# Expert order from four tiles, place rules per expert, and a new order of the last stores and of the first expert products in a hybrid step kernel

## What is computed

```
x = x + gate1 * (mixed @ w_o)
h2 = rms_norm(x, norm2_g) * (1 + scale2) + shift2
x = x + gate2 * hier_moe(h2, ...)

def hier_moe(h, ...):                      # 16 experts in 4 groups, d_expert 512
    g_idx = top-1 group of softmax(t @ w_grp + b_grp)
    top_v, top_i = top-2 experts within that group of t @ w_exp + b_exp
    w_top = softmax(top_v) * g_p
    for e in range(16):
        he = silu(t @ w1[e]) * (t @ w3[e])
        y = y + combine[:, e:e+1] * (he @ w2[e])
```

## Time and profile before

| what | us |
|---|---|
| median of 3 runs | 1240.91 |
| lowest and highest | 1238.01, 1241.13 |
| the profiled execution | 1242.69 |
| its span, first to last instruction | 1240.9 |
| TensorE busy | 1166.9 (94%) |
| VectorE busy | 535.8 (43%) |
| ACT busy | 226.4 (18%) |
| POOL busy | 324.3 (26%) |

### The profile page before, as it was taken

How to read it: one execution, slowest core, us unless ns; L and a number is a source line. 1 busy time by engine, 2 the same in 40 slices (tenths; PEclk the granted TensorE clock), 3 DMA queues, 4 the chain that set the end, 5 groups by cost and what they waited for, 6 DMA issues and landing times.

```text
span 1240.9 us, 14438 instructions
## 1 busy us (share of the span) xinstructions
PE 1166.9 (94%) x5748; PEld 713.9 (58%) x5749; DVE 535.8 (43%) x1037; ACT 226.4 (18%) x478; POOL 324.3 (26%) x269
## 2 busy tenths in 40 slices
PE   4899999999999999999999999999957899999795
PEld 1567677777777777777777777645442233333332
DVE  2553378354786682474244426435650211111111
ACT  3221257222570002001100010021201010101000
POOL 0465600378003333333333333000101111121101
PEclk9999999999999999999999999999868899999998
DMA  9844220022200222222222225441299699999964
GB/s 353 309 159 170 88 77 1 18 68 77 78 1 1 68 68 69 68 68 68 68 68 68 68 70 225 176 170 54 85 382 426 267 352 397 409 405 410 402 210 133
DMA packets 52611, 206.52 MB, mean 166 GB/s; under 512 B 3424, under 2 KB 4000, under 8 KB 46352
## 3 DMA queue, kind: packets, MB, share of 16 engines
q1 hardware_dynamic: 47552, 189.39, 39.8%
q0 software_dynamic: 4672, 15.67, 4.5%
q10 hardware_dynamic: 320, 0.53, 0.1%
HBM read 192.51 MB, written 16.29 MB: 168 GB/s over the span
## 4 chain that ended last, share of the span: by engine, by line
PE 84%; DMA 9%; DVE 2%; issue 1%; POOL 0%; ACT 0%; POOLq 0%; DVEq 0%
PE psum L2222 34%; PE psum L2028 12%; PE psum L2392 6%; PE psum L2286 6%; PE psum L2130 4%; PE psum L2456 3%; PE psum L2418 3%; PE psum L2190 3%; PE psum L2006 3%; PE psum L1948 2%; DMA weight_ring<-in_w 2%; PE psum L2470 2%; DMA arena<-in_w 1%; DMA arena<-rows_scratch 1%; DMA arena<-h_scratch,slot_tokens 1%; PE psum L2164 1%
## 5 line engine op out<-in xcount | busy, mean ns | idle before, releaser
L2222 PE MATMUL psum<-arena,weight_ring 128*128 128x320 f32 x928 | 256.9, 432 | 0.0
L2222 PEld LDWEIGHTS psum<-arena,weight_ring 128*128 128x128 f32 x928 | 175.9, 190 | 72.7
L762 POOL TENSOR_TENSOR weight_ring<-weight_ring 128x512 f32<-128x512 f32 x80 | 105.8, 1323 | 353.6 <-DMA weight_ring<-in_w_in 163.7
L2222 PE MATMUL psum<-x,weight_ring 128*128 128x320 f32 x640 | 179.5, 432 | 0.0
L2222 PEld LDWEIGHTS psum<-x,weight_ring 128*128 128x128 f32 x640 | 121.1, 190 | 49.6
L763 POOL TENSOR_TENSOR weight_ring<-weight_ring 128x512 f32<-128x512 f32 x80 | 110.8, 1386 | 0.0
L1533 DVE TENSOR_TENSOR arena<-psum,arena 128x320 f32<-128x320 f32 x124 | 59.4, 488 | 92.4 <-PE psum L2222 91.6
L2028 PE MATMUL psum<-weight_ring,x 128*128 128x256 f32 x384 | 88.0, 380 | 0.4 <-DVE x L1290 0.4
L2028 PEld LDWEIGHTS psum<-weight_ring,x 128*128 128x128 f32 x384 | 71.7, 190 | 11.2 <-issue 1.1
L2392 PE MATMUL psum<-weight_ring,arena 128*32 128x512 f32 x512 | 78.2, 604 | 0.0
L2286 PE MATMUL psum<-weight_ring,arena 128*128 128x512 f32 x160 | 71.5, 596 | 0.0
(11 more groups left out here) (340 smaller groups left out, 1481.6 us busy)
## 6 DMA issues: line engine op xcount, KB each, us to landing
arena<-in_w SPq DMA_DIRECT2D x22, 2048.0 KB, 17.5
weight_ring<-in_w SPq DMA_DIRECT2D x21, 2048.0 KB, 22.6
weight_ring<-in_w_in SPq DMA_DIRECT2D x16, 2048.0 KB, 8.5
arena<-in_w_ada SPq DMA_DIRECT2D x6, 2048.0 KB, 11.6
x<-in_w SPq DMA_DIRECT2D x5, 2048.0 KB
weight_ring<-in_w_ada SPq DMA_DIRECT2D x8, 1024.0 KB, 14.3
x<-in_x_sample SPq DMA_DIRECT2D x2, 2048.0 KB, 12.1
weight_ring<-in_w_conv_out SPq DMA_DIRECT2D x2, 2048.0 KB, 7.9
```

The costliest lines, as they stand in the source:

```text
L762: nc.gpsimd.tensor_tensor(out[:, 0:2], a_[:, 0:2], b_[:, 0:2], op)
L2222: last = mm(product_psum(q, name), w[:, k, :], src[:, k, :], start=(k == 0), stop=(k == 3))
```

## The change

- The counts matmul no longer is a job of its own. `count(4)` stands inside the last `wo` job, after `rank(3)`, and counts four tiles; `expert_order` uses it and runs before the last `residual`. A second `count(5)` gives the full counts for the overflow chunks only.
- The slot of a token is worked out from five numbers per expert (`rank_distance`, `place_rules`: 16 columns each), which are looked up through the masks of all tokens in one product and one sum of `[128, 800]` (`rules_found`); `places` is left with few steps.
- The first table has 12 columns instead of 92, with one-hots of its own for each tile; the 80 overflow columns move to the weight table, which becomes 184 columns wide (`wide_hots`).
- The last tile's `h2` is shifted by VectorE instead of POOL, POOL's product of it is cut into two halves, and its three stores are issued by ACT instead of SP.
- SP starts with the first weight block right after the order and waits for the last `wo` job only after it. Down blocks of couple 0 wait for `s_last_scaled` and `s_h2out`.
- On TensorE the first gate product comes after the first gathered tile; the weight table and the second tile's transposes follow it. The late modulation part is read by VectorE before the weight table.
- `hidden_half(0)` comes before `gate_difference`.

```diff
@@ psum_jobs
+        if j == 2 * NT - 1:
+            jobs.append(("rank", NT - 2, "dve"))
         jobs.append(("wo", j, "dve"))
...
-    jobs += [("rank", last - 1, "dve"), ("x2T", 2 * last + 1, "act"), ("route", last, "dve"), ("rank", last, "dve")]
-    return jobs + [("count", 0, "dve")]
+    return jobs + [("x2T", 2 * last + 1, "act"), ("route", last, "dve"), ("rank", last, "dve")]
@@ sync
-            job_done(sp, "wo", 2 * NT - 1)
-            sp.wait_ge(s_h2, NT)
-            sp.dma_start(h2_dram[P * CTX:P * NT, :], h2[:, CTX, :]).then_inc(s_h2out, 16)
-            sp.dma_start(y_dram[P * CTX:P * NT, :], x_sb[:, D * CTX:D * NT]).then_inc(s_outx, 16)
-            sp.dma_start(y_dram[T:T + P, :], x_sb[:, D * CTX:D * NT]).then_inc(s_outx, 16)
...
                 load_gate_up("gate", "a", t, a)
+                if t == 0:
+                    job_done(sp, "wo", 2 * NT - 1)
                 load_gate_up("gate", "b", t, b)
...
-                if t == 1:
+                if t == 0:
+                    sp.wait_ge(s_x2, 2 * NT)
+                    sp.wait_ge(s_last_scaled, 1)
+                elif t == 1:
                     sp.wait_ge(s_wtable, NT)
@@ gpsimd
-            pool.wait_ge(s_x2, 2 * NT)
-            nc.gpsimd.tensor_tensor(gate1[:, 0, :], x_sb[:, D * CTX:D * NT], mod2[:, 0, 1, :], mult).then_inc(s_last_wide, 1)
-            pool.wait_ge(s_last_scaled, 1)
-            nc.gpsimd.tensor_tensor(h2[:, CTX, :], h2[:, CTX, :], mod2[:, 1, 1, :], add).then_inc(s_h2, 1)
+            for half in range(2):
+                pool.wait_ge(s_x2, 2 * CTX + half + 1)
+                part = slice(512 * half, 512 * (half + 1))
+                nc.gpsimd.tensor_tensor(gate1[:, 0, part], x_sb[:, D * CTX:D * NT][:, part], mod2[:, 0, 1, part], mult).then_inc(s_last_wide, 1)
@@ scalar
             A(h2[:, CTX, :], gate1[:, 0, :], ACT.Copy, scale=stat[:, 5 * NT - 1:5 * NT]).then_inc(s_last_scaled, 1)
+            act.wait_ge(s_x2, 2 * NT)
+            act.dma_start(y_dram[P * CTX:P * NT, :], x_sb[:, D * CTX:D * NT]).then_inc(s_outx, 16)
+            act.dma_start(y_dram[T:T + P, :], x_sb[:, D * CTX:D * NT]).then_inc(s_outx, 16)
+            act.wait_ge(s_h2, NT)
+            act.dma_start(h2_dram[P * CTX:P * NT, :], h2[:, CTX, :]).then_inc(s_h2out, 16)
@@ vector
+            def place_rules():
+                second, near, far, big, start, cap, step, whole_, past, twice = part16
+                V.tensor_scalar(start, far, 128.0, -64.0, mult, add)
...
+            def rules_found():
+                flat = masks.rearrange("p i j e -> p (i j) e")
+                shape = [P, RULES, 2 * NT, EXPERTS]
+                link(V.tensor_tensor(looked, flat.unsqueeze(1).to_broadcast(shape), rules.unsqueeze(2).to_broadcast(shape), mult))
+                link(V.reduce_sum(found.rearrange("p v n -> p (v n)"), looked.rearrange("p v n e -> p (v n) e"), axis=AX))
 
             def places():
...
+                V.tensor_tensor(passed, rank, found[:, 1], ALU.is_ge)
+                V.tensor_tensor(full, rank, found[:, 3], ALU.is_ge)
+                link(V.tensor_tensor(at_, rank, found[:, 0], add))
...
+            def wide_hots(i):
+                if i >= 2:
+                    dve.wait_ge(s_wtable, i - 1)
+                for j in range(2):
...
+            ranks(NT - 2)
+            expert_order()
             residual(2 * NT - 1)
-            ranks(NT - 2)
+            rank_distance()
+            x2_sum(NT - 1)
+            place_rules()
             x2_rstd(NT - 1)
             dve.sem_inc(s_last_rstd, 1)
             choose(NT - 1)
+            dve.wait_ge(s_last_scaled, 1)
+            h2_shifted(NT - 1)
+            rules_found()
             ranks(NT - 1)
-            expert_order()
             places()
...
             hidden(0)
+            hidden_half(0)
             gate_difference()
             slot_gates(0, 0)
-            hidden_half(0)
             rows_made(0)
@@ tensor
+            def count(tiles):
+                pe.wait_ge(s_upto, tiles)
+                mm(count_psum[tiles - NT + 1], ones[:, :], rt[tiles - 1][:, 48:64], start=True, stop=True).then_inc(s_count, 1)
...
+                if j == 2 * NT - 1:
+                    wo_part(j, ps, 1, range(1))
+                    rank(NT - 2)
+                    count(NT - 1)
+                    wo_part(j, ps, 1, range(1, 4)).then_inc(s_job, 1)
...
-            ada_part(LAST_PAIR, late_psum, range(0, 4), late_slot)
+            ada_part(LAST_PAIR, late_psum, range(0, 2), late_slot)
             rank(NT - 1)
...
-            ada_part(LAST_PAIR, late_psum, range(4, 8), late_slot).then_inc(s_late, 1)
+            count(NT)
+            ada_part(LAST_PAIR, late_psum, range(2, 8), late_slot).then_inc(s_late, 1)
...
-            weight_table()
-            next_tokens(0)
             pe.wait_ge(s_late_rows, 1)
...
-            next_tokens(1)
+            next_tokens(0)
             main_gate(0)
+            pe.wait_ge(s_order, 1)
+            weight_table()
...
+            next_tokens(1)
             main_up(0)
```

More of the change, by code:

```diff
@@ L213 @@
             for j in range(len(JOBS))]
+RULES = 5
 PAIRS = 4
@@ L396, in build @@
         square = at(Z + 16816, 256).rearrange("p (a b) -> p a b", a=16)
-        looked = at(Z + 17072, 2 * NT * EXPERTS).rearrange("p (i e) -> p i e", i=2 * NT)
-        ten = [at(Z + 17232 + 10 * n, 2 * NT) for n in range(17)]
+        rules = at(Z + 17072, RULES * EXPERTS).rearrange("p (v e) -> p v e", v=RULES)
+        found = at(Z + 17152, RULES * 2 * NT).rearrange("p (v n) -> p v n", v=RULES)
+        part16 = [at(Z + 17232 + 16 * n, EXPERTS) for n in range(10)]
+        looked = at(Z, RULES * 2 * NT * EXPERTS).rearrange("p (v n e) -> p v n e", v=RULES, n=2 * NT)
+        ten = [at(Z + 1024 + 10 * n, 2 * NT) for n in range(5)]
         hots = sb("slot_one_hots", (NT - 2) * 2 * SLOTS)
@@ L425, in build @@
         pair = [psum[:, 1024 * j:1024 * (j + 1)] for j in range(PAIRS)]
-        table_psum = pair[PAIRS - 1][:, 512:512 + TABLE]
-        weight_psum = pair[PAIRS - 2][:, 512:512 + TABLE]
+        table_psum = psum[:, 3584:3584 + TILES]
+        wide_psum = psum[:, 2560:2560 + 2 * TABLE]
+        count_psum = [psum[:, 2816 + 16 * n:2832 + 16 * n] for n in range(2)]
         shifted_psum = psum[:, 3840:3904]
@@ L1757, in _ @@
                 if j % 2 == 0:
+                    x2_sum(j // 2 - 1)
                     x2_rstd(j // 2 - 1)
@@ L1783, in _ @@
             V.tensor_copy(idx_out[:, :], rows_out[:, :]).then_inc(s_rows_f, 1)
+            dve.wait_ge(s_lateT, 1)
+            late = late_T_psum.rearrange("p (t l v) -> p l t v", t=4, v=2)
+            for lane, n in enumerate(ADA_PAIRS[LAST_PAIR]):
+                last = V.tensor_tensor(mod[:, 8 * n:8 * n + 8].rearrange("p (n v) -> p n v", v=2), late[:, LANE // 2 * lane],
+                                       col("b_ada")[:, 4 * n:4 * n + 4].unsqueeze(2).to_broadcast([P, 4, 2]), add)
+            last.then_inc(s_late_read, 1)
+            dve.wait_ge(s_late_read, 1)
+            V.tensor_copy(rp[:, 3], m6[:, 5]).then_inc(s_late_mod, 1)
+            dve.wait_ge(s_count, 2)
+            V.tensor_copy(counts, count_psum[1])
             dve.wait_ge(s_rexp, 1)
@@ L2278, in _, with wo_part @@
             pe.wait_ge(s_fev, 6 * last_job + 4)
-            def wo_part(j, ps, part):
+            def wo_part(j, ps, part, steps=range(4)):
                 i, n = divmod(j, 2)
@@ L2284, in wo_part @@
                 pe.wait_ge(s_mixT, 2 + 2 * part)
-                for k in range(4 * part, 4 * part + 4):
+                for k in (4 * part + step for step in steps):
                     last = mm(ps[:, 0:512], mixT[:, k, P * i:P * (i + 1)], w[:, k, :], start=(k == 0), stop=(k == KT - 1))
@@ L2319, in table @@
                 for j in range(2):
-                    last = mm(table_psum, slot_hot[i][:, j, :], pair_hot[i % 2][:, j, :], start=(i == 0 and j == 0),
+                    last = mm(table_psum, slot_hot[i][:, j, :], pair_hot[i][:, j, :], start=(i == 0 and j == 0),
                               stop=(i == NT - 1 and j == 1))
@@ L2369, in weight_table @@
                     for j in range(2):
-                        last = mm(weight_psum, slot_hot[i][:, j, :], pair_hot[i % 2][:, j, :], start=(i == 0 and j == 0),
+                        last = mm(wide_psum, slot_hot[i][:, j, :], wide_hot[i % 2][:, j, :], start=(i == 0 and j == 0),
                                   stop=(i == NT - 1 and j == 1))
```

122 lines of the change are left out of this document (55 added, 67 removed).

## The result

The changed kernel takes **1229.73 us** (median of 4 runs, 1227.84 to 1230.11) where the kernel before takes 1241.02 (1238.01 to 1241.17, 4 runs): ratio 0.991, with an interval of 0.989 to 0.993. It is 11.3 us faster; 13.7 were forecast. The profiled execution took 1229.63 us, its span is 1227.9.

The account below looks back on a forecast made before the run. TensorE and the weight stream together were taken to bound the MoE part. The first down product ends at 974.8 - 0.6 - 11.1 - 2.0 = 961.1, gain 13.7 us, forecast 1227.2 us; 8 in 10 range 1221 to 1234.

Parts of the forecast that it names:

- Part 1: Expert order before the last residual: order at about 885.4, first weight issue at 887.4 against 901.25, stream 14 us earlier.
- Part 2: Last y and h2 stores issued by ACT under the weight stream: h2 issued at 896.0, confirmed at about 908.
- Part 3: Token places and indices: indices at 905.9, h2 store last, first gather issued at 908.3 instead of 910.69, 2.4 us.
- The pairing of packets: Stores beside weight loads: packet for packet, 8 packet pairs per engine and store, 0.77 us a pair.
- the even split: Stores beside weight loads: a split evenly by bytes, as a bound, confirms the h2 store at about 901.
- Part 4: TensorE's order: gate product after first gather, 8.9 us; table 4.9 us before the up product; 0.6 us left.
- Part 5: hidden_half(0) ahead of gate_difference(): 11.06 us wait and 2.0 us low clock go; gate rows land near 960, cover 10 us.
- (a): Rival: front end cheaper, with stores split evenly, gate product at full clock, table 4 us; about 1222; chance 0.17.
- (b): Rival: the table on TensorE's path costs its long bound and the clock falls; about 1233; chance 0.13.
- (c): Rival: stream doesn't follow, starved stores delay SP's fourth block and gathers; h2 down at 918 gives 1237; chance 0.06.
- (d): Rival: slower, low clock from 922.6 on in the first products, 30 us lost; 1243 to 1257; chance 0.03.
- (e): Rival: slower, tokens over the places start the overflow loop, 40 us or more; chance 0.01.

Follow-up runs that it names:

- e3: The changed kernel with SP's first weight block also waiting for VectorE's first one-hots, so that the weight stream starts late; 1228.29 us.
- e7: The kernel before with hidden_half(0) ahead of gate_difference() and the first gate product ahead of the second gathered tile's transposes; 1227.71 us.
- e8: e6 with the added line of e3, so that the weight stream starts late; 1232.29 us.
- e6: The changed kernel with the edits of e4 and e5 together; 1221.57 us.
- e5: The changed kernel with the last h2 store ahead of the two y stores, and SP's fourth block no longer waiting for these; 1227.02 us.
- e4: The changed kernel with the weight table put back under the first gather, ahead of the first gathered tile; 1225.25 us.
- e2: The changed kernel with hidden_half(0) put back behind gate_difference() and slot_gates(0, 0); 1229.62 us.
- e1: The kernel before with one edit, hidden_half(0) moved ahead of gate_difference() and slot_gates(0, 0); 1228.39 us.

## Why the prediction was right, and where it was not

**The mechanism was right.** I said that the end of the first down product sets the rest, one to one. Where no product but that of couple 6 waits for a block, the rest is 263.6 to 266.3 us in seven kernels whose fronts differ by up to 18.5 (the kernel before has one more wait, of 0.6). The rule ends where the stream is late: e3, e7 and e8, with a start at 901 to 904 and fronts of 77 to 82, have 267.9, 267.9 and 275.6.

**Part 1** held. With the 1.85 us between the two starts of `choose(3)` added, the order was made at 885.3 (885.4 forecast) and the first block issued at 887.0 (887.4). What the early start is worth I had not asked, and e3 and e8 answer: in the changed kernel nothing that shows (1.4 us the other way, inside the noise), as three blocks ahead fill the buffers by 942 and the loads slow the stores; in e6, with five blocks ahead and a front 7 us shorter, 8 to 11 us.

**Part 2 holds the term that was mis-sized.** I had the h2 store issued at 896.0 and confirmed at about 908, in 12 us. It was issued in time (895.7 by the same count) but took 14.03 us, and POOL issued 0.79 later. So the first gather came 33.5 us after `choose(3)`, against 33.6 before: of the 2.4 us of part 3 about 0.1 were left, and this is the greater part of the 13.7 that came out as 11.2. The pairing of packets was right. ACT's stores are queue q10, SP's loads q1, from 892 to 895 us (packets, MB, share of 16 engines; from 898 to 901 it is 72 packets beside 70):

```profile
q1 hardware_dynamic: 67, 0.98, 78.8%
q10 hardware_dynamic: 66, 0.27, 21.9%
```

Packet for packet, but a load's packet is nearly four times a store's. What I had too short is the stretch of the y stores: I had them and the three blocks through at 905.5, and SP's fourth block, which waits for them, went out at 906.89, or 908.7 by the same count; the h2 store landed 1.0 behind that. The 14.0 us need both causes: without the y stores ahead of it the store takes 10.22 beside full loads (e5), and without the loads 3.0, the y stores then being down before it is issued (e3). So the loads cost it most, some 7 us, and the y stores 3.8 on top.

The Trainium skill (DMA: Bandwidth & Descriptors, section SWDGE vs HWDGE vs iDMA) says that a DMA engine goes round its internal queues in turn, and prefers packets of at most 4096 B. The turns agree with the trace, 67 packets beside 66. The size doesn't for the loads, 0.98 MB in 67 packets or 14.6 KB each, and the even split that I kept as a bound did not come.

**Part 3** was right in its times: indices at 904.51, or 906.4 (905.9 forecast). One step of `choose(3)` (L1682, 0.79 us instead of 0.23) and one of `place_rules` were held beside POOL's two halves of the product; this is the second:

```profile
885.00 1.27 POOL L863 TENSOR_TENSOR arena<-x,arena 128x512 f32<-128x512 f32 x1 [8.53 <-DVE x L1640]
```
```profile
885.12 1.19 DVE L1730 SCALAR_TENSOR_TENSOR arena<-arena 128x16 f32<-128x16 f32 x1
```

Both steps end with POOL's instruction (876.5 and 886.3); undisturbed the second takes 0.17. The Trainium skill (SBUF — State Buffer, section Who interferes with whom) says that a VectorE instruction with two inputs in SBUF contends with a GpSimd one that reads SBUF, and that the one that was issued first decides who is blocked; for L1730, issued 0.12 us behind POOL's, the trace agrees. The hold in `choose(3)` cost nothing, as VectorE waits for TensorE behind it (0.59 us, at 880.49). The one in `place_rules` lies on the chain that leads to the h2 store and the first gather (885.12, shown above), so up to 1.0 us of the front is POOL's; no run takes it away.

**Part 4** held to 0.2 us a step: 8.69 us for the gate product at first at the low clock (8.9), 4.9 for the table (4.9). That the table was hidden in its old place I had written down, but I had not priced leaving it there: that is 4.5 us more than the change gives (e4), where I booked 0.6 us for everything up to the up product.

**Part 5** was right in the gain, 11.06 + 1.96 us, and wrong in the reason that it needed. I had the rows land near 960 and a cover of 10 us for `hidden(1)`; they came about 10 us sooner (in e2, whose front is the same up to there, at 950.9), through a hole in the stream that I did not see. I had the stream run on to 957 (28.3 MB at 425 GB/s from 888.2 end at 954.8 already), but SP's next issue waited for the end of the up product (945.68). So the moved `hidden_half(0)`, which I had priced at 13 us, is worth nothing beside the other parts (e2), and all of it without them (e1). With either cause the product ends at the same place, so the sum was near without having tested the reason that it gave.

**The rivals.** (a), a cheaper front, did not come: the stores were not split evenly, and the table took its 4.9 us. e6 measures its 1222, but by two other edits, so that the number agrees by chance. (b) fell: the granted clock was 0.90 already from 926 to 930, and the table kept its 4.9. (c) had 2 us of truth, the late h2 store; no product waited for the stream. Neither (d) nor (e) showed.

## What to carry to other kernels

Before a chain of edits is made to shorten a front, test the one that removes the last wait alone: here one moved line gave 12.3 us, as much as the whole change. Let a transfer that sets a start go out first in its queue (2.7 us here), and put table work under a gather, not between two products (4.5 us). Measure the head start of a stream in the final kernel, not in the one you start from: here it was worth nothing with three blocks ahead and a long front, and 8 to 11 us with five blocks ahead and a short one.

## What the hardware showed that I had not expected

- A read-back of two times 512 KB on POOL's queue took 17.1 us beside a full stream (the kernel before, 944.79 to 961.87) and 5.7 us in a hole of the stream (e2, 945.23 to 950.89).
- From 985 to 1085 us a DMA share of 1.00 stood for 389 to 392 GB/s (the kernel before, the changed one, e2, e4, e5, e6) and one of 1.01 or 1.02 for 402 to 406 (e1, e3, e7, e8). A share that reads full had another 3% in it.
- A 512 KB store took 3.0 us without loads (e3), 10.2 beside a saturated load queue as the first in its own (e5), and 14.0 behind 1 MB of stores (the changed kernel). Packets took turns, not bytes: the loads' queue, with 14.6 KB a packet, had 78.8% of the engines' time, the stores' with 4 KB 21.9%.
